# Router as weights on four column groups, and the second expert's weights behind the landing of the first expert's rows

## The chip, the core and the metric

The kernel runs on one core of a Trainium2 chip. The metric is the device time of one execution in microseconds (us). The kernel before takes 1316.21 us, the median of three runs (1314.29 to 1318.43). One further execution was profiled. Its device time is 1313.54 us, and its span, from the first to the last record, is 1311.7 us. All row times below are counted from the start of that span.

## The reference

One layer of a hybrid decoder over 1024 prompt tokens and 8 x 4 sample tokens, of width 1024, all in float32. The first part of the layer (an RWKV-7 recurrence beside windowed attention) is only touched at its loads. What matters here begins with the output projection and the mixture of experts:

```python
x = x + (mixed @ prm['w_out'])                       # 1056 tokens x 1024
h2 = rmsnorm(x, prm['norm_ffn_g'])
pg = softmax(h2 @ prm['w_route_group'] + prm['b_route_group'])         # 4 groups
le = h2 @ prm['w_route_expert'] + prm['b_route_expert']                # 16 experts
# the best group of each token, then the best two of its four experts
y = silu(xb @ w_gate[e]) * (xb @ w_up[e]) @ w_down[e]                  # 1024 -> 512 -> 1024
x = x + sum of the two experts' rows, each by its weight
```

So the router is a product of each token's row h2 (1024 values) with 20 columns: 4 of `w_route_group` and 16 of `w_route_expert`.

## The kernel before

Each engine (TensorE, VectorE, ScalarE, GpSimd, and SyncE, which issues most DMAs) has one instruction stream written out by hand, and semaphores order them. `F32` products need two passes of the array, so each `matmul` or `transpose` leaves two load records and two matmul records where both passes are recorded for it; the counts below are counts of records.

The 1056 tokens are 9 tiles: eight of 128 tokens and one of 32. In the stage that the change touches, TensorE goes through the tiles t = 0 to 8 in this order: the output projection of tile t + 2 (`project`, `w_part`, L1146; the last tile, t = 8, is projected in L1153 on four column groups of the array with 32 tokens each); eight transposes of the normalised rows h2 of tile t (L1214) into PSUM banks 2 and 6; a wait until ScalarE has copied them to `h2T` (`turned_rows`, L1676); and eight products for the router (L1220). In these, a block of `h2T` (128 x 128) is loaded as weights and the 20 columns of `wr20` are moved through, and the eight sum up in bank 3. Beside it, VectorE adds the projected rows to the residual (L2189), ScalarE takes the mean square (`mean_square`, L1666 to L1668), VectorE writes h2 (L2198, L2199), and SyncE stores h2 and x to DRAM (L561, L562). On ScalarE the mean square of tile t + 1 stands ahead of the copies of tile t; for the last tile, four copies (L1686) first bring its projection out of PSUM after t = 6, and its mean square stands behind the copies of t = 7.

After the last router product VectorE works out the choice of experts for all tokens (L2218 to L2262) and, with TensorE (L1292, L1299, L1301), the lists of token numbers for each expert, `idxA` for 128 rows and `idxB` for up to 32 more. GpSimd then gathers the rows of the experts from DRAM with indirect DMAs (L2493), into two slots. Once the first expert's rows have landed (`xg0` at 32: both gathers), TensorE turns them (`turn`, L1239 and L1245), and goes on with gate and up (`gate_up`, L1258), the turn of the next expert, and down (`down`, L1277; L1283 on four column groups). All 16 experts follow this pattern.

An expert's weights are three transfers of 2 MB (`load_expert`, L568), into one of two slots. SyncE issues those of the first two experts together, as soon as h2 and x are stored:

```python
for a in range(2):
    load_expert(EO[a], a)
```

Those of expert n + 2 are issued once `down` of expert n is done. The gathers and the weights use the same 16 DMA engines, on different queues (the gathers on q0, SyncE's transfers on q1).

The router's weights, its bias and the gain `gffn` are loaded by SyncE in L538 to L542, once `ryl_ok` says that the arena below them is free. Behind them on SyncE stand two small outputs, the load of the residual tile 3 (L548), that of the tiles 4 to 7 (L551), and later the stores. `fs_dve` reaches 2 with the product of L2109. At the start of the kernel SyncE loads, under three semaphores, the small LoRA matrices (`lora_in`), the level masks (`level_in`) and the caches and biases (`bias_in`); TensorE, GpSimd, VectorE wait for them.

Of the kernel before, what the change touches and what calls it, by code (L numbers as in the profile page):

```python
# [13 lines left out]
P = 128  # L14
# [49 lines left out]
SEMS = """consts vecs_in lora_in shift_in pad_zero x0 x1 x2 x3 sumsq ms_ok std_ok h_ok hT_ps hT_ok vec_ps vec_ok w0 w1 w2 p_ps p_ok  # L64
shT_ps shT_ok prev_ok dve mixed lora_act lora_ps gates_ok kk_sq kk_ps kk_ms kk_std bonus_in bonus_ps exps scaled
kbt_ok blk_done tails_ok ptail_ps ptail_ok sh_out win_out ptail_out smp_ps smp_ok cum_ok
kvs_ok bias_in level_in level_ok sc_ps sc_ok m_ok e_ok p_norm pt_ps pt_ok ob_ps ob_ok gam_ok gamma_ok
# [4 lines left out]
ln_ok fs_pe fs_dve fs_act f_mean f_yc f_sq f_var f_std f_gate f_sc f_mx wo_in x2_in g_in g_ps g_x2 g_lg  # L72
# [5 lines left out]
def constants():  # L78
# [12 lines left out]
    table = np.concatenate([ident, head_ones, head_ones / HD, strict, m64, eye64, ones, iota, tokid, tokid < TOK, -(TOK + i[:, None]), -4 * (TOK + P + i[:, None] % 32), i[:, None] // 32], axis=1)  # L91
# [27 lines left out]
TABLE = ["ident", "head_ones", "head_mean", "strict", "m64", "eye64", "ones", "iota", "tokid", "valid", "spareA", "spareB", "quarter"]  # L119
TABLE_W = dict(ident=P, head_ones=P, head_mean=P, strict=P, m64=P, eye64=HD, ones=P, iota=CAP, tokid=NT + 1, valid=NT + 1, spareA=1, spareB=1, quarter=1)  # L120
# [4 lines left out]
def program(nc, i, o):  # L125

    ctx = ExitStack()
    with ctx:
# [133 lines left out]
        wr20 = part(F0 + 8192 + 2 * D, KB * 20).rearrange("p (b n) -> p b n", b=KB)  # L262
        rbias = part(F0 + 8192 + 2 * D + 160, 20)
        R0 = F0 + 8192 + 2 * D + 180
# [47 lines left out]
        R0 += 2 * TD  # L312
        OHX = part(R0, 2 * NTT * 3 * NE).rearrange("p (m a e) -> p m a e", m=2 * NTT, a=3)
# [91 lines left out]
        def _(sp):  # L405
# [47 lines left out]
            sp.dma_start(wlora[0:HD, :], i["w_decay_up"][0]).then_inc(s["lora_in"], 16)  # L453
            sp.dma_start(wlora[HD:P, :], i["w_iclr_up"][0]).then_inc(s["lora_in"], 16)
            sp.dma_start(wgate[:, :], i["w_gate_up"][0]).then_inc(s["lora_in"], 16)
            load_w(2)
            sp.dma_start(levelf, i["c_level"]).then_inc(s["level_in"], 16)
# [81 lines left out]
            sp.dma_start(wr20[:, :, 0:NG], i["w_route_group"][0].rearrange("(b p) n -> p b n", p=P)).then_inc(s["g_in"], 16)  # L539
# [35 lines left out]
            for a in range(2):  # L575
                load_expert(EO[a], a)
# [63 lines left out]
        def _(pe):  # L640
# [559 lines left out]
            for t in range(2):  # L1200
                for hf in range(2):
                    last = w_part(t, hf, 7)
                last.then_inc(s["g_ps"], 1)
# [1375 lines left out]
```

## Time and profile before

| | before |
|---|---|
| median of three runs | 1316.21 us (1314.29 to 1318.43) |
| device time of the profiled execution | 1313.54 us |
| its span | 1311.7 us |
| TensorE busy | 1193.5 us (91%) |
| VectorE busy | 468.4 us (36%) |
| ScalarE busy | 360.0 us (27%) |
| mean granted clock of TensorE | 0.957 of full |
| DMA traffic | 176.00 MB, mean 134 GB/s |

The profile page gives busy times over the whole span, and then the span in 40 slices of 32.8 us. The chain of waits follows the work that ended last back to what released each step; its pieces add up to the span, so a piece that is on it and gets shorter shortens the span, as long as nothing else then ends later. The timeline shows instructions in order of time with the idle time before them. In the table of windows the column PEclk is the clock granted to TensorE, 1.00 for 2.4 GHz and 0.50 for 1.2 GHz.

### The profile page before, as it was taken

What the parts mean: (1) busy time and instruction counts of PE and PEld (TensorE: products, weight loads), DVE (VectorE), ACT (ScalarE), POOL (GpSimd) and SP (SyncE); (2) the same over time, 40 slices, a digit from 0 to 9 for tenths busy, and PEclk for the clock granted to TensorE, in tenths of its full rate; (3) what the DMA queues carried; (4) which work ended last, traced back from release to release, by engine and by line L of the source; (5) the groups of instructions that cost most, each with busy time, mean ns of one, the idle gap of its engine ahead of it and who ended that gap; (6) DMA issues with size and microseconds to landing.
All of it is one profiled execution on the core that took longest, in us unless ns stands there. A gap on an engine that the chain in (4) does not pass through costs nothing.

```text
span 1311.7 us, 25299 instructions
## 1 busy us (share of the span) xinstructions
PE 1193.5 (91%) x11136; PEld 852.6 (65%) x11136; DVE 468.4 (36%) x921; ACT 360.0 (27%) x784; POOL 289.1 (22%) x171
## 2 busy tenths in 40 slices
PE   6999999999998877687899998499999999999995
PEld 4666666555665666475544455388887888877884
DVE  4201575377555766666242112500010100011133
ACT  3102555434342554524112112111111011111052
POOL 0000000011101899996000000111111121121203
PEclk8999999999999989988799998599999999999998
DMA  6412000110104000021405102949887788887983
GB/s 204 124 33 69 16 17 18 32 36 21 36 16 59 7 4 3 3 51 38 150 16 187 64 32 93 354 158 277 289 294 260 238 281 270 291 292 252 329 324 127
DMA packets 97194, 176.00 MB, mean 134 GB/s; under 512 B 20403, under 2 KB 42350, under 8 KB 96693
## 3 DMA queue, kind: packets, MB, share of 16 engines
q1 hardware_dynamic: 88548, 152.04, 34.4%
q0 software_dynamic: 8544, 22.51, 6.6%
q8 instruction: 75, 1.23, 0.4%
q14 instruction: 27, 0.21, 0.1%
HBM read 148.89 MB, written 29.06 MB: 136 GB/s over the span
## 4 chain that ended last, share of the span: by engine, by line
PE 83%; DVE 10%; issue 3%; ACT 2%; DMA 1%; SPq 0%; POOLq 0%; POOL 0%; DVEq 0%; ACTq 0%
PE ps L1258 22%; PE ps L674 21%; PE ps L1146 9%; PE ps L1277 9%; PE ps L1283 2%; PE ps L1220 1%; PE ps L753 1%; DVE arena L2018 1%; PE ps L777 1%; PE ps L766 1%; PE ps L1239 1%; PE ps L1245 1%; PE ps L1070 1%; DVE arena L1999 1%; PE ps L1062 1%
## 5 line engine op out<-in xcount | busy, mean ns | idle before, releaser
L674 PE MATMUL ps<-arena 128*128 128x355 f32 x960 | 299.8, 469 | 2.8 <-issue 2.6
L1258 PE MATMUL ps<-arena 128*128 128x160 f32 x2048 | 284.8, 301 | 0.8 <-issue 0.6
L1258 PEld LDWEIGHTS ps<-arena 128*128 128x128 f32 x2048 | 280.9, 191 | 7.1 <-issue 7.1
L674 PEld LDWEIGHTS ps<-arena 128*128 128x128 f32 x960 | 180.3, 191 | 108.3 <-issue 11.2
L1146 PE MATMUL ps<-arena 128*128 128x512 f32 x256 | 120.3, 619 | 0.7 <-DVE arena L2091 0.7
L1277 PE MATMUL ps<-arena 128*128 128x512 f32 x256 | 114.6, 599 | 0.7 <-DVE arena L2273 0.7
L2273 DVE TENSOR_TENSOR arena<-arena,ps 128x160 f32<-128x160 f32 x64 | 20.5, 321 | 254.1 <-ACT arena L1711 254.1
L2493 POOL DMA_INDIRECT arena<-h_dram,idxA x16 | 16.1, 1005 | 430.9 <-DVE idxB L2304 221.8
L1711 ACT ACTIVATE arena<-ps 128x160 f32<-128x160 f32 x64 | 19.5, 304 | 327.0 <-PE ps L1258 327.0
L1146 PEld LDWEIGHTS ps<-arena 128*128 128x128 f32 x256 | 49.3, 198 | 58.6 <-issue 56.8
L2434 POOL TENSOR_TENSOR arena<-arena 128x1024 f32<-128x1024 f32 x4 | 11.4, 2859 | 340.6 <-DVE arena L1895 340.6
L1277 PEld LDWEIGHTS ps<-arena 128*128 128x128 f32 x256 | 47.2, 190 | 54.6 <-issue 53.0
L1368 ACT COPY arena<-ps 128x355 f32<-128x355 f32 x60 | 27.2, 453 | 183.7 <-PE ps L674 183.7
L2486 POOL DMA_INDIRECT x_dram<-arena,rowA x13 | 20.9, 1606 | 94.6 <-DVE arena L2283 94.6
L2454 POOL TENSOR_TENSOR arena<-arena 128x1024 f32<-128x1024 f32 (+4 forms) x40 | 41.0, 1026 | 2.8
L2281 DVE TENSOR_SCALAR arena<-ps,arena 128x512 f32<-128x512 f32 x13 | 9.8, 751 | 87.1 <-PE ps L1277 87.1
L921 PE MATMUL ps<-arena 64*64 64x64 f32 x1280 | 33.1, 242 | 4.3 <-DVE arena L2018 4.3
L2189 DVE TENSOR_TENSOR arena<-arena,ps 128x1024 f32<-128x1024 f32 x8 | 9.8, 1220 | 76.2 <-PE ps L1146 76.2
L1676 ACT COPY arena<-ps 128x512 f32<-128x512 f32 (+1 forms) x18 | 9.1, 553 | 94.7 <-PE ps L1214 94.7
L1435 ACT ACTIVATE arena<-arena 128x256 f32<-128x256 f32 (+1 forms) x64 | 30.9, 485 | 12.6 <-DVE arena L1930 12.6
L1924 DVE SCALAR_TENSOR_TENSOR arena<-ps,arena 128x1024 f32<-128x1024 f32 (+1 forms) x16 | 18.5, 1158 | 42.0 <-PE ps L753 42.0
L2018 DVE COPY_PREDICATED arena<-level,ps 128x512 f32<-128x512 uint8 x32 | 22.7, 710 | 29.6 <-PE ps L933 29.6
(390 smaller groups left out, 1656.9 us busy)
## 6 DMA issues: line engine op xcount, KB each, us to landing
arena<-in_w_exp_gate SPq DMA_DIRECT2D x16, 2048.0 KB, 12.6
arena<-in_w_exp_up SPq DMA_DIRECT2D x16, 2048.0 KB, 17.5
arena<-in_w_exp_down SPq DMA_DIRECT2D x16, 2048.0 KB, 21.9
arena<-in_w_in SPq DMA_DIRECT2D x16, 512.0 KB, 3.8
arena<-in_x_prompt SPq DMA_DIRECT2D x9, 512.0 KB, 4.3
x_dram<-arena SPq DMA_DIRECT2D x9, 512.0 KB, 3.6
h_dram<-arena SPq DMA_DIRECT2D x8, 512.0 KB, 2.6
out_y_prompt<-arena SPq DMA_DIRECT2D x8, 512.0 KB, 2.8
```

The lines of the kernel that those rows point to most:

```text
L674: last = pe.matmul(ps[:, q % 2, 0:m], wr[:, n % 3, k, :], hT[:, k, a:a + m], start=(k == 0), stop=(k == KB - 1))
L921: last = pe.matmul(ps[row(e ^ u), 4 * b + u, j * CH:(j + 1) * CH], LB[row(e), b, u, j, 0:CH], TL[row(e), b, JB * u + j, :], start=True, st ...
L1146: return pe.matmul(ps[0:n, 4 * (t % 2) + hf, :], MX[:, b, t * P:t * P + n], wo[b][:, hf * 512:(hf + 1) * 512], start=(b == 0), stop=(b == 7))
L1258: last = pe.matmul(ps[:, 3 + f % 2, n * CAP:(n + 1) * CAP], w[a][:, k, f * P:(f + 1) * P], xgT[:, a, k, :], start=(k == 0), stop=(k == KB ...
L1277: last = pe.matmul(ps[:, 5 + n, :], eact[:, a, k, 0:P], edown[a][:, k, n * 512:(n + 1) * 512], start=(k == 0), stop=(k == 3))
L1283: last = pe.matmul(ps[j * XB:(j + 1) * XB, 7, 0:TD], eact[:, a, k, P:CAP], edown[a][:, k, j * TD:(j + 1) * TD], start=(k == 0), stop=(k == ...
L1368: act.copy(pT[:, pos, a:a + m], ps[:, q % 2, 0:m]).then_inc(s["p_ok"], 1)
L1435: last = act.activation(sc[:, u % 2, g, a:], sc[:, u % 2, g, a:], ACT.Exp, bias=ast[:, 4 * (u % 2) + g:4 * (u % 2) + g + 1], accum_out=ast ...
L2018: dve.copy_predicated(TL[:, b].rearrange("p (u j) t -> p u j t", u=2), lm(lv, 0, 2 * JB).rearrange("p (u j) t -> p u j t", u=2), ps[:, 4 * ...
L2273: dve.tensor_tensor(eact[:, a, f, :], egl[:, f % 2, :], ps[:, 3 + f % 2, CAP:2 * CAP], ALU.mult).then_inc(s["ac_ok"], 1)
L2454: link(pool.tensor_tensor(stm[:, :, 0:m], stm[:, :, 0:m], stm[:, :, m:2 * m], ALU.add))
L2486: pool.indirect_dma_start(dst, bass.IndirectOffsetOnAxis(rows[:, EO[e]:EO[e] + 1], 0), src[:, e % 2, :], None, compute_op=ALU.add).then_in ...
```

## The change

The router's weights become the stationary side. `wr32` holds 32 columns for each of the eight blocks of 128 rows (20 of them the router's and 12 of zeros, which GpSimd writes). The block k is loaded on column group k mod 4 of the array, and 128 tokens of `h2T` are moved through it; the eight products leave four partial sums of 32 rows each, stacked in the 128 partitions of bank 7. ScalarE copies them to `lT`, and one more product per tile, with `lT` as weights and a 0/1 matrix `stack` (128 x 20) moved, sums the four parts and turns them back, into the same place in bank 3. This product of tile t stands behind the transposes of tile t + 1. `g_lt` counts the partial sums, `g_lt_ok` the copies, and `g_lg` the finished logits as before. The loads of the router's weights and bias, and the write of zeros, wait in addition for `fs_dve` at 2. `wr32` is 96 words wider than `wr20`, and what lies behind it in the arena moves up.

SyncE issues the second expert's weights only when `xg0` is at 32, that is, when both gathers of the first expert have landed. The first expert's are issued as before.

To free two semaphores, the loads of `lora_in` and `level_in` count on `bias_in` as well, and each of the four that wait for one of the three now waits for all 12 transfers. The table of constants grows by the 20 columns of `stack`.

```diff
-        wr20 = part(F0 + 8192 + 2 * D, KB * 20).rearrange("p (b n) -> p b n", b=KB)
-        rbias = part(F0 + 8192 + 2 * D + 160, 20)
-        R0 = F0 + 8192 + 2 * D + 180
+        wr32 = part(F0 + 8192 + 2 * D, KB * 32).rearrange("p (b n) -> p b n", b=KB)
+        rbias = part(F0 + 8192 + 2 * D + 256, 20)
+        R0 = F0 + 8192 + 2 * D + 276
...
+        lT = part(R0, 2 * P).rearrange("p (s t) -> p s t", s=2)
...
             sp.wait_ge(s["ryl_ok"], NB_ * HP)
             sp.dma_start(gffn, i["norm_ffn_g"].to_broadcast([P, D])).then_inc(s["g_in"], 16)
-            sp.dma_start(wr20[:, :, 0:NG], i["w_route_group"][0].rearrange("(b p) n -> p b n", p=P)).then_inc(s["g_in"], 16)
-            sp.dma_start(wr20[:, :, NG:NG + NE], i["w_route_expert"][0].rearrange("(b p) n -> p b n", p=P)).then_inc(s["g_in"], 16)
+            sp.wait_ge(s["fs_dve"], 2)
+            sp.dma_start(wr32[:, :, 0:NG], i["w_route_group"][0].rearrange("(b p) n -> p b n", p=P)).then_inc(s["g_in"], 16)
+            sp.dma_start(wr32[:, :, NG:NG + NE], i["w_route_expert"][0].rearrange("(b p) n -> p b n", p=P)).then_inc(s["g_in"], 16)
...
             for a in range(2):
+                if a:
+                    sp.wait_ge(s["xg0"], 32)
                 load_expert(EO[a], a)
...
-                    pe.wait_ge(s["lora_in"], 48)
+                    pe.wait_ge(s["bias_in"], 16 * 12)
...
+            def logits(t):
+                n = toks(t)
+                pe.wait_ge(s["g_lt_ok"], t + 1)
+                pe.matmul(ps[0:n, 3, t * 20:(t + 1) * 20], lT[:, t % 2, 0:n], T["stack"], start=True, stop=True).then_inc(s["g_lg"], 1)
...
+                if t:
+                    logits(t - 1)
                 pe.wait_ge(s["hT_ok"], 2 * NTT + 2 * t + 2)
                 if t == 0:
-                    pe.wait_ge(s["g_in"], 16 * 5)
+                    pe.wait_ge(s["g_in"], 16 * 5 + 1)
                 for k in range(KB):
-                    last = pe.matmul(ps[0:n, 3, t * 20:(t + 1) * 20], h2T[:, t % 2, k, 0:n], wr20[:, k, :], start=(k == 0), stop=(k == KB - 1))
-                last.then_inc(s["g_lg"], 1)
+                    j = k % 4 * 32
+                    last = pe.matmul(ps[j:j + 32, 7, 0:n], wr32[:, k, :], h2T[:, t % 2, k, 0:n], start=(k < 4), stop=(k >= 4), tile_position=(0, j))
+                last.then_inc(s["g_lt"], 1)
+            logits(NT)
...
                     if t >= 2:
-                        act.wait_ge(s["g_lg"], t - 1)
+                        act.wait_ge(s["g_lt"], t - 1)
...
                 turned_rows(t)
+                act.wait_ge(s["g_lt"], t + 1)
+                if t >= 2:
+                    act.wait_ge(s["g_lg"], t - 1)
+                act.copy(lT[:, t % 2, 0:toks(t)], ps[:, 7, 0:toks(t)]).then_inc(s["g_lt_ok"], 1)
...
-            pool.wait_ge(s["level_in"], 16)
+            pool.wait_ge(s["bias_in"], 16 * 12)
...
+            pool.wait_ge(s["ryl_ok"], NB_ * HP)
+            pool.wait_ge(s["fs_dve"], 2)
+            pool.memset(wr32[:, :, NG + NE:], 0.0).then_inc(s["g_in"], 1)
```

## Rows read from the trace of the kernel before

**Rows 1.** The profile page: TensorE's busy time; its granted clock in 40 slices.
```profile
PE 1193.5 (91%) x11136; PEld 852.6 (65%) x11136; DVE 468.4 (36%) x921; ACT 360.0 (27%) x784; POOL 289.1 (22%) x171
...
PEclk8999999999999989988799998599999999999998
```

**Rows 2.** Waits, TensorE, 880 to 1290 us: in total, times, longest.
```profile
PE ps L1277 <- DVE arena L2273: 0.7, 1, 0.7
```

**Rows 3.** Chain of waits, 680 to 880 us: start us, us, what.
```profile
713.19 15.50 PE ps L1146 x32
...
746.08 0.45 PE ps L1214 x4
...
747.67 1.96 PE ps L1220 x16
749.64 15.52 PE ps L1146 x32
...
768.72 13.82 PE ps L1146 x32
...
803.49 3.59 PE ps L1153 x64
```

**Rows 4.** Views of single lines: ns min/median/max, first and last start in us.
```profile
L1153 PEld LDWEIGHTS ps<-arena x64: 107/110/110, 803.4 to 806.5; 128*32 128x32 f32 x64
...
L1301 PE MATMUL ps<-table,arena x8: 206/218/231, 834.4 to 834.5; 128*32 128x48 f32 x8
...
L1299 PE MATMUL ps<-table,arena x2: 275/292/310, 834.1 to 834.2; 128*128 128x48 f32 x2
```

**Rows 5.** Windows of 1 us: busy time of each engine, PEclk, DMA share, GB/s.
```profile
713.00:714.00 1.00, 1.00 (x3) 0.50 (x3) 1.00 (x1) 0.00 (x0) 0.00 (x0) 0.51 0.00 0
...
767.00:768.00 1.00, 1.00 (x11) 1.00 (x11) 0.00 (x0) 0.97 (x3) 0.00 (x0) 1.00 0.00 0
812.00:813.00 1.00, 0.56 (x3) 0.56 (x3) 0.00 (x0) 1.00 (x2) 0.00 (x0) 0.50 0.00 0
```

**Rows 6.** Timeline, 799 to 821 us: start, us, engine, line [idle before].
```profile
808.67 1.49 ACT L1686 COPY arena<-ps 32x256 f32<-32x256 f32 x4
...
812.27 1.05 ACT L1666 ACTIVATE arena<-arena 32x1024 f32<-32x1024 f32 x1
812.44 3.60 PE L1220 MATMUL ps<-arena 128*128 128x20 f32 x16 [0.73 <-ACT arena L1676]
...
814.01 1.27 DVE L2199 SCALAR_TENSOR_TENSOR arena<-arena,stat 32x1024 f32<-32x1024 f32 x1
...
815.97 1.06 PE L1214 MATMUL ps<-table,arena 32*128 32x32 f32 x8
...
818.53 0.33 DVE L2218 TENSOR_TENSOR arena<-ps,arena 128x160 f32<-128x160 f32 x1 [2.80 <-PE ps L1220]
```

**Rows 7.** Chain of waits, 834 to 880 us.
```profile
837.12 7.61 DMA arena<-h_dram,idxB
...
878.69 1.42 PE ps L1258 x9
```

**Rows 8.** Timeline row; DMA issues (820 us, 837 us, 872 us): us to landing; L568's landings.
```profile
820.97 4.37 SPq L568 DMA_DIRECT2D arena<-in_w_exp_down  x1
...
arena<-in_w_exp_down SPq DMA_DIRECT2D x1, 2048.0 KB, 18.4
...
arena<-h_dram,idxB POOLq DMA_INDIRECT x1, 7.6
...
arena<-h_dram,idxB POOLq DMA_INDIRECT x1, 4.0
...
DMA to landing us min/median/max: 8.9/17.5/29.7
```

**Rows 9.** Timeline, 678 to 693 us: VectorE's L2109 and SyncE's L551.
```profile
678.89 0.28 DVE L2109 TENSOR_TENSOR arena<-yS,ps 128x128 f32<-128x128 f32 x1
...
692.15 0.41 SPq L551 DMA_DIRECT2D arena<-in_x_prompt  x1
```

More of the change, by code:

```diff
@@ L62 @@
 ARENA = 20 * W + KB * W + HP * W1 + 15504
-SEMS = """consts vecs_in lora_in shift_in pad_zero x0 x1 x2 x3 sumsq ms_ok std_ok h_ok hT_ps hT_ok vec_ps vec_ok w0 w1 w2 p_ps p_ok
+SEMS = """consts vecs_in shift_in pad_zero x0 x1 x2 x3 sumsq ms_ok std_ok h_ok hT_ps hT_ok vec_ps vec_ok w0 w1 w2 p_ps p_ok
 shT_ps shT_ok prev_ok dve mixed lora_act lora_ps gates_ok kk_sq kk_ps kk_ms kk_std bonus_in bonus_ps exps scaled
 kbt_ok blk_done tails_ok ptail_ps ptail_ok sh_out win_out ptail_out smp_ps smp_ok cum_ok
-kvs_ok bias_in level_in level_ok sc_ps sc_ok m_ok e_ok p_norm pt_ps pt_ok ob_ps ob_ok gam_ok gamma_ok
+kvs_ok bias_in level_ok sc_ps sc_ok m_ok e_ok p_norm pt_ps pt_ok ob_ps ob_ok gam_ok gamma_ok
 rt_ps rt_act rt_dve r_eye rl_ps rl_ok rc_ps rc_ok rg_ps rg_ok ru_ps ru_ok rx_ps rx_ok rxt_ps rxt_ok rm_ps rm_ok
@@ L71 @@
 sv_out sv_in pool sr_ok sy_out sy_in st_out
-ln_ok fs_pe fs_dve fs_act f_mean f_yc f_sq f_var f_std f_gate f_sc f_mx wo_in x2_in g_in g_ps g_x2 g_lg
+ln_ok fs_pe fs_dve fs_act f_mean f_yc f_sq f_var f_std f_gate f_sc f_mx wo_in x2_in g_in g_ps g_x2 g_lt g_lt_ok g_lg
 h2o0 h2o1 hot hot_ps i_ok n_rounds
@@ L90, in constants @@
     tokid = i[:, None] + P * tile_[None, :]
-    table = np.concatenate([ident, head_ones, head_ones / HD, strict, m64, eye64, ones, iota, tokid, tokid < TOK, -(TOK + i[:, None]), -4 * (TOK + P + i[:, None] % 32), i[:, None] // 32], axis=1)
+    table = np.concatenate([ident, head_ones, head_ones / HD, strict, m64, eye64, ones, iota, tokid, tokid < TOK, -(TOK + i[:, None]), -4 * (TOK + P + i[:, None] % 32), i[:, None] // 32, i[:, None] % 32 == np.arange(20)[None, :]], axis=1)
     levels = []
@@ L116, in constants @@
             "c_sbias": sbias.astype(np.float32)}
-TABLE = ["ident", "head_ones", "head_mean", "strict", "m64", "eye64", "ones", "iota", "tokid", "valid", "spareA", "spareB", "quarter"]
-TABLE_W = dict(ident=P, head_ones=P, head_mean=P, strict=P, m64=P, eye64=HD, ones=P, iota=CAP, tokid=NT + 1, valid=NT + 1, spareA=1, spareB=1, quarter=1)
+TABLE = ["ident", "head_ones", "head_mean", "strict", "m64", "eye64", "ones", "iota", "tokid", "valid", "spareA", "spareB", "quarter", "stack"]
+TABLE_W = dict(ident=P, head_ones=P, head_mean=P, strict=P, m64=P, eye64=HD, ones=P, iota=CAP, tokid=NT + 1, valid=NT + 1, spareA=1, spareB=1, quarter=1, stack=20)
 VECS = ["norm_mix_g", "mu_shift", "w_decay0", "w_iclr0", "k_k", "k_a", "r_k", "lnx_g", "lnx_b", "attn_norm_g"]
@@ L452, in _ @@
             sp.dma_start(shin[:, :], i["state_shift"][0]).then_inc(s["shift_in"], 16)
-            sp.dma_start(wlora[0:HD, :], i["w_decay_up"][0]).then_inc(s["lora_in"], 16)
-            sp.dma_start(wlora[HD:P, :], i["w_iclr_up"][0]).then_inc(s["lora_in"], 16)
-            sp.dma_start(wgate[:, :], i["w_gate_up"][0]).then_inc(s["lora_in"], 16)
+            sp.dma_start(wlora[0:HD, :], i["w_decay_up"][0]).then_inc(s["bias_in"], 16)
+            sp.dma_start(wlora[HD:P, :], i["w_iclr_up"][0]).then_inc(s["bias_in"], 16)
+            sp.dma_start(wgate[:, :], i["w_gate_up"][0]).then_inc(s["bias_in"], 16)
             load_w(2)
-            sp.dma_start(levelf, i["c_level"]).then_inc(s["level_in"], 16)
+            sp.dma_start(levelf, i["c_level"]).then_inc(s["bias_in"], 16)
             for dst, src in ((kc, "cache_win_k"), (vc, "cache_win_v")):
@@ L782, in s_cache @@
             def s_cache(n):
-                pe.wait_ge(s["bias_in"], 16 * 8)
+                pe.wait_ge(s["bias_in"], 16 * 12)
                 pe.wait_ge(s["sa_act"], 1 + n)
@@ L1955, in _ @@
             link(dve.memset(pn[:, :, 0:1], 0.0))
-            dve.wait_ge(s["bias_in"], 16 * 8)
+            dve.wait_ge(s["bias_in"], 16 * 12)
             for k in range(NU + 1):
@@ L2193, in _ @@
                 if t == 0:
-                    dve.wait_ge(s["g_in"], 16 * 5)
+                    dve.wait_ge(s["g_in"], 16 * 5 + 1)
                 if t >= 2:
```

## The prediction

> **What bounds the kernel now.** I read the page first. TensorE is busy 91% of the span, and its granted clock is full in most slices but not in those around 700 to 760 us and 790 to 850 us [rows 1]. The next view is the waits of TensorE behind 880 us: in the whole phase of the experts the longest is 0.7 us, once [rows 2]. That phase is TensorE's own work, and the change does not touch it; whatever is won ahead of it moves its start and is kept. So the question is what stands on the chain of waits between 700 and 880 us. There the chain is nearly all TensorE: projection of a tile, transposes, a wait for ScalarE's copies, and the router's 16 records, again and again [rows 3]. Then comes VectorE's choice of experts, and then one DMA, the gather of the first expert's last rows, at 7.61 us [rows 7]. The change aims at the router's records and at this gather.
>
> **The router, tiles 0 to 5.** The 16 records of a tile take 1.96 us on the chain [rows 3], 0.123 us each, for only 20 moved columns; they are paid for by the loads of 128 columns of weights. After the change 32 columns are loaded and 128 moved, on four column groups. The nearest row is L1153, which also has loads of 32 columns on four groups, but moves 256: 64 records in 3.59 us [rows 3], 0.056 us each. Half the columns should take half of that, 0.028 us, if columns set the price: 16 x 0.028 = 0.45 us. The other bound comes from eight records of L1301, 48 columns wide, whose starts lie within 0.1 us [rows 4], about 0.015 us each, which shows that the loads of 32 columns alone allow 0.24 us. From above, 16 x 0.056 = 0.90 us. I take 0.6 us, the half of L1153 and 0.15 us for going into the column groups and out of them, as an estimate: the 3.59 us of L1153 hold two such changes and leave little more than that over its smooth part. The gain is 1.96 - 0.6 = 1.37 us a tile (bounds 1.07 and 1.6), and six tiles (0 to 5) are followed by a projection, so that it stays on the chain: 8.2 us (6.4 to 9.6).
>
> The added product of each tile costs two records with 128 columns of weights; the like of L1299 has two in about 0.4 us [rows 4]. It stands behind the next tile's transposes, where TensorE waits for ScalarE anyway: from the end of the transposes at 746.53 to the router at 747.67 it is idle for 1.14 us [rows 3]. So it costs nothing for tiles 0 to 7; without that cover it would be 0.4 us a tile, 3 us in all. ScalarE's added copy (128 x 128, below 0.3 us) comes before its mean square of a later tile, which is not needed for more than 10 us, since a projection of 13.8 us stands in between.
>
> **The clock.** The same 32 records of a projection take 15.50 and 15.52 us behind tiles 0 and 2, and 13.82 us behind tile 3 (and also behind 1 and 4) [rows 3]. The windows show why: at 713 us and again at 751 us the granted clock is 0.5, that is 1.2 GHz, for 3.4 us, while it stays at 1.0 behind the other tiles [rows 5]. What TensorE did before these falls is always the same: transposes, 1.14 us of idling, and 2 us of products that move 20 columns. After the change the idling has a product in it, and the router takes a third of the time with four groups at work on 128 columns, so the stretch of little work shrinks from 3.6 us to about 2.2 us. I expect the two falls to go: 1.68 + 1.70 = 3.4 us. The bounds are 0 (they stay, or come at other tiles instead) and 3.4.
>
> **The last tiles.** Here no projection is left to hide anything. Before, from the start of the transposes of tile 6 (807.01) to VectorE's first step on the logits (818.53) it is 11.5 us [rows 6]. I go through it anew. The router of tile 6 ends 1.4 us earlier, but ScalarE now copies its parts (0.3 us) before the four copies of L1686 (1.49 us), which end at 4.25 instead of 3.15 us from the start; only then does it copy the transposes of tile 7, to 5.3 us, just as before. The router of tile 7 ran at the low clock in 3.60 us [rows 6]; now it ends at about 6.0 to 6.4 us. That gain is not kept: the mean square of tile 8 used to run beside it, and now stands behind the copy of tile 7's parts on ScalarE. It begins at 6.3 to 6.7 us, takes 1.5 us, and VectorE's two steps another 1.5 (1.27 of them L2199), so the transposes of tile 8 begin at 9.3 to 9.7 us instead of 8.96 us. Behind them, the copies take 1.4 us, the router 0.5 instead of 1.04 us, then the new copy 0.35 us and the last product 0.4 us, which nothing hides any more. Sum: 12.0 to 12.5 us against 11.5. The tail loses 0.8 us (0.5 to 1.3). The falls of the clock in the tail I leave as they are: at 812 us it is at 0.5 [rows 5], and stretches of waiting remain.
>
> **The gather.** The two experts' weights, 12.6 MB, are issued from 820 us on and fill the DMA engines until about 855 us. The gather of `idxB` is issued at 837.12 and lands after 7.6 us; the same gather at 872 us, with no weights under way, lands after 4.0 us [rows 7, 8]. After the change only the first expert's 6.3 MB stand ahead. Its last transfer lands 18.4 us after its issue at 820.97, at 839.4 [rows 8]; since the stores of the last tile come 0.4 us later against VectorE's steps, at 839.8. Until then the gathers share, and from then they are alone: some 0.4 MB of the 0.66 MB are left, 1 us at the engines' rate, and then the landing. I put the landing of `idxB` at 841.4 instead of 844.7, a gain of 3.3 us. Bounds: 3.6 us (the undisturbed 4.0) from above, and 2 us if the first expert's transfers hold the rows up longer. The first expert's weights have landed before gate and up need them, 3.6 us after the rows.
>
> The second expert's weights are then issued at 841.4 us, 21 us later than before. They are needed at 878.69 - 3.3 = 875.4 us [rows 7], 34 us later. With nothing queued ahead, the three of the first expert took 18.4 us to the last landing, and the longest landing of any is 29.7 us, which was with 12.6 MB queued [rows 8]. So nothing waits for them, with 4 us to spare in the worst case and 15 us in the likely one. Behind the new wait on SyncE stand only the third expert's weights, which wait for the first `down` anyway, and TensorE and GpSimd need nothing of that queue sooner.
>
> **The waits for 12 transfers and for `fs_dve`.** `fs_dve` is at 2 at 679.2 us [rows 9], 39 us after the router's weights were loaded before. Five issues and two small outputs take about 5 us on SyncE, so the residual tile 3 is issued near 685 us and not at 675.6, and lands by 689; L551 behind it waits for VectorE until 692.15 us [rows 9] and is not moved. The router's weights land near 689 us, and TensorE wants them at 711 us, VectorE the bias of `g_in` near 698 us. Cost 0; the cover is 9 us. The merged waits cost 0 too: the last of the 12 loads is issued at 40 us and the level masks and LoRA weights are used behind 240 us. GpSimd has been idle since 613 us when it writes the zeros. The table's 10 KB more are below what the vectors' loads behind it take.
>
> **The sum.** 8.2 + 3.4 - 0.8 + 3.3 = 14.1 us. Against the profiled execution, 1313.54 - 14.1 = 1299.4 us; the median of the runs is 2.7 us above it, so 1316.2 - 14.1 = 1302.1 us.
>
> **Rivals.**
> (a) The falls of the clock stay or move to other tiles. For it: they depend on where they strike among like tiles (two of six before). Against it: the stretch of little work is shorter by a third. 10.7 us, 1305.5 us.
> (b) Loads set the router's price, not columns. Each load of 32 columns lasts 0.110 us [rows 4]; if they could not overlap, 16 would take 1.76 us, the gain would be 0.2 us a tile, and the total 14.1 - 8.2 + 1.2 = 7.1 us, 1309.1 us. Against it: L1153 has 64 of them in 3.59 us, so they do overlap.
> The Trainium skill ("TensorE: Matmul & The Clock Gate", Back-to-back issue gap) gives about 81 ns for each pair of load and matmul in a sustained stream at 128 moved columns; that would be an estimate of 1.3 us a tile and a gain of 4 us in place of 8.2. By that rule the time would be some 4 us above my forecast; no row before shows 128 columns on four groups.
> (c) The gather waits for something other than the weights, and its 7.6 us stay. For it: its own issue and the second expert's gathers are near. Against it: 4.0 us when alone. 10.8 us, 1305.4 us.
> (d) Slower: the second expert's weights come too late for its `gate_up` at 875.4 us. Every us beyond 34 us from issue to landing is paid in full, and the kernel is slower than before from 48 us on; at 52 us it would be 1302.1 + 18 = 1320 us. Against it: no landing beyond 29.7 us.
> (e) Slower by nothing, faster by nothing: several of (a) to (c) at once, near 1312 us.
>
> **How the numbers follow.** Forecast 0.62, (a) 0.14, (b) 0.10, (c) 0.06, (d) 0.03, (e) 0.05. The forecast's own bounds are 6.4 to 9.6 for the router, 0.5 to 1.3 for the tail, 2 to 3.6 for the gather; with some 2 us for the runs' spread they reach from 1298 to 1307, and that holds (a) and (c) as well, some 8 in 10. A measurement of this kernel can tell about 0.3%, 4 us. Faster by more than that: the forecast, (a), (b), (c): 0.92. Same: (e), 0.05. Slower: (d), 0.03.
>
> **What the next profile would show.** The chain has 16 records of the router in 0.5 to 0.7 us a tile (0.9 or more speaks for (b)). All projections behind tiles 0 to 4 take 13.8 us (15.5 anywhere is (a)). From the transposes of tile 6 to VectorE's first step it is 12.0 to 12.5 us. The gather of `idxB` lands 4 to 5 us after its issue (7.6 is (c)). TensorE does not wait for the second expert's weights; if it does, (d). A wait of TensorE or VectorE for `g_in` near 700 us, or idling between the column groups and the projection, would make the sum wrong in a place that I put at nothing.

## The result, and the profile after

The changed kernel takes 1303.81 us in the median of six runs (1301.74 to 1310.42), the kernel before, measured beside it, 1317.29 us (1313.31 to 1318.95). The ratio is 0.9931 with a 95% interval of 0.9908 to 0.9954: 9.1 us less of 1316.21, between 6.1 and 12.1. That makes 1307.1 us against a forecast of 1302.1 us, 0.1 us beyond the upper end of its range (1298 to 1307 us). The profiled execution has a span of 1301.7 us, 10.0 us below that of before. The same changed kernel run once more later (e11 below) gave 0.9915 (0.9886 to 0.9943).

The page of the kernel after, first the row of busy times, then TensorE's granted clock in 40 slices:

```profile
PE 1182.3 (91%) x11154; PEld 843.4 (65%) x11154; DVE 468.9 (36%) x921; ACT 361.8 (28%) x793; POOL 289.1 (22%) x172
...
PEclk9999999999999989888899998599999999999998
```

TensorE is busy for 11.2 us less than in [rows 1]. The chain of waits of the kernel after, 680 to 875 us (start us, us, what), holds the rest of the story; L1150 is the projection, L1232 the router's parts, L1223 the transposes, L1157 the projection of the last tile, L2235 VectorE's first step on the logits, L1305 the lists of tokens, L1271 gate and up:

```profile
694.16 17.43 PE ps L1150 x40
...
713.19 0.64 PE ps L1232 x16
713.84 13.93 PE ps L1150 x32
...
794.71 3.45 PE ps L1157 x64
798.17 0.60 PE ps L1223 x4
...
804.40 1.05 ACT arena L1679 x2
...
810.05 0.34 DVE arena L2235
...
820.88 5.27 PE ps L1305 x36
...
829.62 5.20 DMA arena<-h_dram,idxB
...
838.52 20.02 PE ps L1271 x128
```

The router takes 0.64 us a tile where [rows 3] has 1.96 us. Each of the five projections behind tiles 0 to 4 takes 13.93 us: none is at 15.5 us as two were in [rows 3], and none is at the 13.82 us of the others. The gather of `idxB` lands after 5.20 us, not 7.61 us [rows 7].

The same chain of the kernel before, beside [rows 3] and [rows 7] (L1292 are the lists of tokens, L1258 gate and up):

```profile
692.17 17.43 PE ps L1146 x40
...
807.08 0.60 PE ps L1214 x4
...
829.37 4.29 PE ps L1292 x36
...
848.44 19.84 PE ps L1258 x128
```

A stage that starts and ends at the same work in every version makes the kernels comparable. I use the stretch from the transposes of tile 0 to the first expert's gate and up. Before, it goes from 709.60 (the last piece of the projection ahead of the transposes of tile 0 begins at 692.17 and takes 17.43 us) to 848.44: 138.84 us. After, it goes from 711.59 to 838.52: 126.93 us, which is 11.91 us less. The remaining difference lies outside it: the stage begins 1.99 us later after, and the experts' phase behind it is within 0.1 us of what it was.

### The profile page after: what moved, and what is told of

The parts are those of the page before. It is cut to its first block, busy times and chain, and to the rows that moved or that the text cites. A ratio compares the mean times of both kernels' runs of the same rounds, so it can differ in the third digit from the quotient of the medians.

```text
span 1301.7 us, 25353 instructions
## 1 busy us (share of the span) xinstructions
PE 1182.3 (91%) x11154; PEld 843.4 (65%) x11154; DVE 468.9 (36%) x921; ACT 361.8 (28%) x793; POOL 289.1 (22%) x172
## 4 chain that ended last, share of the span: by engine, by line
PE 83%; DVE 10%; issue 3%; ACT 3%; DMA 1%; SPq 0%; POOLq 0%; POOL 0%; DVEq 0%; ACTq 0%
PE ps L1271 22%; PE ps L678 21%; PE ps L1290 9%; PE ps L1150 9%; PE ps L1296 2%; PE ps L757 1%; DVE arena L2035 1%; PE ps L781 1%; PE ps L770 1%; PE ps L1252 1%; PE ps L1074 1%; PE ps L1258 1%; PE ps L937 1%; PE ps L946 1%; DVE arena L2016 1%
## 5 line engine op out<-in xcount | busy, mean ns | idle before, releaser
L1271 PE MATMUL ps<-arena 128*128 128x160 f32 x2048 | 285.1, 301 | 0.6 <-issue 0.6
L1271 PEld LDWEIGHTS ps<-arena 128*128 128x128 f32 x2048 | 281.0, 191 | 6.9 <-issue 6.9
L1150 PE MATMUL ps<-arena 128*128 128x512 f32 x256 | 115.1, 597 | 0.7 <-DVE arena L2108 0.7
L1290 PE MATMUL ps<-arena 128*128 128x512 f32 x256 | 114.6, 599 | 0.7 <-DVE arena L2290 0.7
L1150 PEld LDWEIGHTS ps<-arena 128*128 128x128 f32 x256 | 47.4, 190 | 56.8 <-issue 55.1
L1013 PEld LDWEIGHTS ps<-arena 64*64 64x64 f32 x240 | 13.2, 145 | 29.3 <-DVE arena L2055 17.4
```

Source lines behind the costliest of these rows:

```text
L1150: return pe.matmul(ps[0:n, 4 * (t % 2) + hf, :], MX[:, b, t * P:t * P + n], wo[b][:, hf * 512:(hf + 1) * 512], start=(b == 0), stop=(b == 7))
L1271: last = pe.matmul(ps[:, 3 + f % 2, n * CAP:(n + 1) * CAP], w[a][:, k, f * P:(f + 1) * P], xgT[:, a, k, :], start=(k == 0), stop=(k == KB ...
L1290: last = pe.matmul(ps[:, 5 + n, :], eact[:, a, k, 0:P], edown[a][:, k, n * 512:(n + 1) * 512], start=(k == 0), stop=(k == 3))
```

## The experiments

Stage lengths below are all from the transposes of tile 0 to the first gate and up, each from one profiled execution. Where no ratio is given (e5 to e8 and e10), the kernel was run once, and the profiled execution is that run.

**e1: the changed kernel without the wait for the rows.**

```diff
             for a in range(2):
-                if a:
-                    sp.wait_ge(s["xg0"], 32)
                 load_expert(EO[a], a)
```

> The changed kernel without its wait for the first expert's rows: both experts' weights are issued together, as before. Theory (the router and the gather are two separate gains): the sum of the trace after is about -11 us for the router with the clock, +0.4 for the tail, -2.4 for the gather, so this kernel should be 7 to 9 us faster than before, and 2 to 3 us slower than the changed kernel, with the gather of idxB landing about 7.6 us after its issue again. All projections behind tiles 0 to 4 take 13.8 to 13.9 us. Rival (the gather is not slowed by the second expert's weights): it is as fast as the changed kernel, and idxB lands after 5 us.

Measured: ratio 0.9915 (0.9887 to 0.9944). Chain of waits of e1:

```profile
710.62 13.93 PE ps L1148 x32
...
825.72 6.90 DMA arena<-h_dram,idxB
...
836.32 20.33 PE ps L1269 x128
```

The stage goes from 708.37 to 836.32, 127.95 us: 10.9 us shorter than before without the wait. The expectation was right on the gather being slow again (6.90 us) and wrong on how much the wait adds: the changed kernel's stage is only 1.0 us shorter than this one, not 2 to 3 us, and the two ratios cannot be told apart.

**e2: the kernel before with the wait alone.**

```diff
             for a in range(2):
+                if a:
+                    sp.wait_ge(s["xg0"], 32)
                 load_expert(EO[a], a)
```

> The kernel before with only the wait for the first expert's rows ahead of the second expert's weights. Theory: idxB lands after 5 us and not 7.6 us, the kernel is 2 to 3 us faster than before, and one to three of the projections behind tiles 0 to 5 take about 15.5 us, since the router is the old one. Rival (the wait is worth nothing or makes the second expert late): within 0.5 us of before, or a wait of TensorE for the second expert's weights.

Measured: ratio 0.9952 (0.9932 to 0.9972), 6.3 us less (3.7 to 9.0). Chain of waits of e2:

```profile
713.84 15.20 PE ps L1148 x32
732.61 15.52 PE ps L1148 x32
...
829.72 5.27 PE ps L1294 x36
...
838.71 3.65 DMA arena<-h_dram,idxB
...
846.19 19.30 PE ps L1260 x128
```

The wait alone brings the gather's own row from 7.61 to 3.65 us, 4.0 us. The stage, 709.97 to 846.19, is 136.22 us, only 2.6 us shorter than before. The row overstates the gain: the token lists took 5.27 us here against 4.29 us, so that this gather was issued later. The measure that holds is from VectorE's first step on the logits to the landing of `idxB`: 26.2 us before (818.53 to 844.73), 23.5 us here (818.89 to 842.36). On top of the router the wait gains 1.0 us by the same measure: 25.8 us in e1, 24.8 us after and 24.9 us in e11. So the two halves of the change don't add up. The times give the wait alone 6.3 us, and even the lower end of their interval, 3.7 us, is above the 2.6 us of the stage; where the rest lies is open.

A part of the reason is in the next view.

The timeline row in which SyncE issues the last of the first expert's weights, of the kernel after, and the us from that issue to landing:

```profile
813.46 3.96 SPq L570 DMA_DIRECT2D arena<-in_w_exp_down  x1
...
arena<-in_w_exp_down SPq DMA_DIRECT2D x1, 2048.0 KB, 19.3
```

Before, this issue stood 2.44 us behind VectorE's first step on the logits (818.53 and 820.97, [rows 6, 8]); after, 3.41 us (810.05 and 813.46). The weights wait for the stores of tile 8, which wait for its mean square. The first of these stores was issued 3.2 us ahead of VectorE's first step before and 2.7 us ahead of it after, which is half of the 1.0 us; the other half is that the weights were issued 3.77 us behind the last store's issue and not 3.30 us, for which no run shows a cause. Then the transfer itself took 19.3 us to its landing, where it took 18.4 us before. It took 19.2 to 20.2 us in all six executions with the new products in which all of the first expert's weights are issued ahead of the gather (after, e1, e5, e6, e10, e11), and 18.4 to 18.6 us in the four without them; the cause is open too. So the first expert's weights land at 832.76, 3.1 us behind the issue of the gather at 829.62. In the kernel before, where the second expert's weights follow at once, the first's landed at 839.4, 2.3 us behind the issue at 837.12.

**e3: what is left of the change without the new products and without the wait.** The router multiplies as before, by 20 of the 32 columns.

```diff
-                if a:
-                    sp.wait_ge(s["xg0"], 32)
...
-                    j = k % 4 * 32
-                    last = pe.matmul(ps[j:j + 32, 7, 0:n], wr32[:, k, :], h2T[:, t % 2, k, 0:n], start=(k < 4), stop=(k >= 4), tile_position=(0, j))
-                last.then_inc(s["g_lt"], 1)
-            logits(NT)
+                    last = pe.matmul(ps[0:n, 3, t * 20:(t + 1) * 20], h2T[:, t % 2, k, 0:n], wr32[:, k, 0:20], start=(k == 0), stop=(k == KB - 1))
+                last.then_inc(s["g_lg"], 1)
...
-                act.copy(lT[:, t % 2, 0:toks(t)], ps[:, 7, 0:toks(t)]).then_inc(s["g_lt_ok"], 1)
```

> What is left of the change without the router's new products and without the wait for the rows: merged semaphores, the wider table and wr32 in the arena, the loads of the router's weights behind fs_dve, the zeros. The router multiplies as before, by 20 of the 32 columns. Theory (the 2 us that the trace after loses ahead of 693 us are the clock's falls striking at other places in this one execution, not the change): the ratio to before is 1.000 within 0.002, and the stages ahead of 693 us come out within 2 us of before, either way. Rival (the merged waits or the table cost time): 1.5 to 3 us slower than before, and the start of the output projection's last part comes 2 us later in its trace.

Measured: ratio 0.9996 (0.9974 to 1.0018). Chain of waits of e3:

```profile
712.11 15.52 PE ps L1148 x32
...
765.96 15.52 PE ps L1148 x32
...
836.13 7.05 DMA arena<-h_dram,idxB
```

The stage is 138.34 us (708.54 to 846.88), as before within 0.5 us. The merged semaphores, the wider table, the moved arena and the wait for `fs_dve` cost nothing that shows. The timeline of the kernel after agrees: the load of the residual tile 3 (L550) is issued at 684.05, 10 us before L553, the load of tiles 4 to 7, which still goes as soon as VectorE allows it.

```profile
684.05 0.36 SPq L550 DMA_DIRECT2D arena<-in_x_prompt  x1
694.13 0.41 SPq L553 DMA_DIRECT2D arena<-in_x_prompt  x1
```

**e4: the kernel before, unchanged.**

> The kernel before, unchanged, as a kernel of its own: how far a comparison of a kernel with itself is from 1, and how far stages differ between two profiled executions of one program. Theory (the clock's falls strike differently from one execution to the next): ratio 1.000 within 0.002; the falls behind the router's tiles come at other tiles or in another number than behind tiles 0 and 2, each at 1.7 us, and the stages ahead of 693 us differ by 1 to 3 us. Rival (they are fixed by the program): again 15.5 us behind tiles 0 and 2 alone, and the stages ahead within 0.5 us.

Measured: ratio 0.9996 (0.9973 to 1.0019). Chain of waits of e4:

```profile
688.53 17.43 PE ps L1146 x40
...
709.73 15.31 PE ps L1146 x32
...
745.99 15.52 PE ps L1146 x32
...
825.73 4.20 PE ps L1292 x36
...
833.41 7.34 DMA arena<-h_dram,idxB
```

The stage is 138.48 us (705.97 to 844.45), 0.4 us from the first profiled execution, but it begins 3.6 us earlier (688.53 against 692.17 for its last projection piece). So one program's stages ahead of it differ by that much between executions. The falls came behind tiles 0 and 2 again, which the rival expected; but in e3 and e2, whose TensorE work here is the same, they came behind tiles 0 and 3, and 0 and 1. All four have two falls among the five, one of them behind tile 0; the place of the other is not fixed.

**e10: the old router's products beside the new ones.** They go into columns of bank 3 that nobody reads.

```diff
+                for k in range(KB):
+                    pe.matmul(ps[0:n, 3, 256:276], h2T[:, t % 2, k, 0:n], wr32[:, k, 0:20], start=(k == 0), stop=(k == KB - 1))
                 for k in range(KB):
                     j = k % 4 * 32
```

> The changed kernel, in which TensorE also does the old router products (16 records of 20 moved columns a tile) ahead of the new ones, into columns of bank 3 that nobody reads. It tells what of the old router goes with the falls of the clock. Theory (the falls come with the long stretch of light work: transposes, idling and products of 20 columns): about 2.6 us a tile for the router's lines instead of 0.64, and the falls are back, so that one to three of the projections behind tiles 0 to 5 take 15.2 to 15.6 us. Rival (the new products at the end of the stretch are enough to hold the clock): all of them take 13.8 to 13.9 us.

Measured: 1327.39 us in one run. Chain of waits of e10 (L1231 the old products, L1234 the new):

```profile
715.86 16.48 PE ps L1150 x32
...
733.93 1.96 PE ps L1231 x16
735.90 0.57 PE ps L1234 x16
...
754.54 15.63 PE ps L1150 x32
...
792.37 15.63 PE ps L1150 x32
```

With the old products back, the falls are back: 16.48, 15.63 and 15.63 us behind tiles 0, 2 and 4, and 13.93 behind the other two. The new products at the end of the stretch don't hold the clock. Together with the eight profiled executions without the old products (after, e1, e5 to e9, e11), in which all 40 projections took 13.93 us, and the four with the old ones alone (before, e2 to e4), two falls in each, this shows that the falls went with the old router's products. It does not tell whether their few moved columns do it or the time that they take: from the transposes to the next projection it is 3.6 us before and 4.1 us in e10, with falls, and 2.2 us after and 2.7 us in e6, without. No run has a long way there without the old products.

**e6: the new products twice.**

```diff
-                for k in range(KB):
+                for k in [*range(KB), *range(KB)]:
                     j = k % 4 * 32
```

> The changed kernel with the eight products of the router's parts issued twice for each tile (the second time over the first, the same result). It measures the price of 16 more records. Theory (moved columns set the price): 16 x 0.027 = 0.43 us more, 1.07 us a tile instead of 0.64. Rival 1 (loads or a fixed price per record, 0.64 / 16 = 0.040 us): 1.28 us a tile. Rival 2 (loads of 0.110 us do not overlap, or the Trainium skill's 81 ns a pair): 1.9 us or more. The projections stay at 13.9 us in all three.

Measured: chain of waits of e6:

```profile
719.95 1.08 PE ps L1232 x32
```

Sixteen more records cost 0.44 us, 0.0275 us each. The loads of 0.110 us one behind the other, 0.081 us a pair and 0.040 us a record are out by this number. That columns set it takes a second row, since e6 adds columns and records alike: L1153, with the same loads and 256 columns, takes 0.056 us a record [rows 3], twice as much. It is also a fourth of what the full array takes: the projection moves 512 columns a record in 0.432 us (13.82 / 32, [rows 3]), which is 0.108 us for 128. The other 0.20 us of the 0.64 are not in the price of a record and are paid once a tile; that they are the way into the column groups is argued. The rows of the last projection agree: it takes 3.59 us [rows 3] behind products on the full array and 3.45 us (L1157) behind the new ones, 0.14 us less.

**e5: ScalarE's order of the last tiles.** The four copies of the last projection ahead of the copy of tile 6's parts, the mean square of tile 8 ahead of the copy of tile 7's.

```diff
                 turned_rows(t)
-                act.wait_ge(s["g_lt"], t + 1)
-                if t >= 2:
-                    act.wait_ge(s["g_lg"], t - 1)
-                act.copy(lT[:, t % 2, 0:toks(t)], ps[:, 7, 0:toks(t)]).then_inc(s["g_lt_ok"], 1)
                 if t + 1 == NT - 1:
...
                 if t + 1 == NT:
                     mean_square(NT)
+                act.wait_ge(s["g_lt"], t + 1)
+                if t >= 2:
+                    act.wait_ge(s["g_lg"], t - 1)
+                act.copy(lT[:, t % 2, 0:toks(t)], ps[:, 7, 0:toks(t)]).then_inc(s["g_lt_ok"], 1)
```

> The changed kernel with ScalarE's order of the last tiles changed: the four copies of the last tile's projection ahead of the copy of tile 6's parts, and the mean square of tile 8 ahead of the copy of tile 7's parts. Theory (the tail is longer than before because ScalarE's copies of the parts stand ahead of the mean square of tile 8): from the transposes of tile 6 to VectorE's first step on the logits it is 11.88 us in the changed kernel and should be 10.4 to 10.8 us here. Rival (the tail is set by TensorE and the last copy and product): 11.7 to 12.0 us.

Measured: span 1299.2 us. Chain of waits of e5 (L1679 is the mean square of tile 8):

```profile
796.65 0.60 PE ps L1223 x4
...
801.07 1.16 ACT arena L1679 x2
...
806.83 0.34 DVE arena L2235
```

From the transposes of tile 6 to the logits it is 10.18 us, a little below what was expected, against 11.88 us in the kernel after: the mean square begins 4.42 us behind the transposes instead of 6.23 us. So ScalarE's order was what made the tail longer. But the stage is only 1.4 us shorter (125.48 us, 710.07 to 835.55). The gather took 6.34 us, 1.1 us more than after, while the token lists took 4.37 us, 0.9 us less: it was issued earlier, and the first expert's weights were under way beside it for longer. From the logits to the landing of `idxB` it is 25.0 us.

**e7: the first expert's down weights also behind its rows.**

```diff
...
-            for a in range(2):
-                if a:
-                    sp.wait_ge(s["xg0"], 32)
-                load_expert(EO[a], a)
+            load_expert(EO[0], 0, slice(0, 2))
+            sp.wait_ge(s["xg0"], 32)
+            sp.wait_ge(s["w0"], w_total(18) + 32)
+            load_expert(EO[0], 0, slice(2, 3))
+            load_expert(EO[1], 1)
...
-                pe.wait_ge(s[f"w{a}"], WBASE[a] + 24 * g + (48 - 24 * a))
+                pe.wait_ge(s[f"w{a}"], WBASE[a] + (32 if a == 0 and first else 24 * g + (48 - 24 * a)))
...
+                if first:
+                    pe.wait_ge(s["w0"], WBASE[0] + 48)
```

> The changed kernel with the third transfer of the first expert's weights (down, 2 MB) also behind the landing of its rows; down waits for it by itself. Theory (the gather of idxB takes 5.2 us in the changed kernel because the first expert's last transfer is still under way): it lands 3.6 to 4.1 us after its issue, 1.1 to 1.6 us earlier, and nobody waits for down's weights, which land some 9 us after and are needed 20 us after. Rival (the 5.2 us are the gather's own): 5.0 to 5.3 us again.

Measured: span 1300.4 us. Chain of waits of e7, and the landing of the down weights:

```profile
829.59 3.92 DMA arena<-h_dram,idxB
...
arena<-in_w_exp_down SPq DMA_DIRECT2D x1, 2048.0 KB, 9.0
```

The gather lands after 3.92 us, and nobody waits for the down weights. The stage is 124.87 us (712.33 to 837.20), 2.1 us shorter than after; 1.3 us of it is the gather, 0.8 us the token lists, which here took 4.49 us instead of 5.27. So what was left of the gather's delay was the first expert's own third transfer. Here the shorter lists count, because nothing holds up the gather that follows them: from the logits to the landing of `idxB` it is 22.7 us. In e11 the lists took the same 4.49 us, and it is 24.9 us, 0.1 us more than after.

**e8: both experts' weights behind the rows.**

```diff
             for a in range(2):
-                if a:
+                if not a:
                     sp.wait_ge(s["xg0"], 32)
                 load_expert(EO[a], a)
```

> The changed kernel with the weights of both first experts behind the landing of the first expert's rows: no weights at all are under way when the rows are gathered, and the first expert's weights come late. It measures the gather alone and the price of late weights. Theory: idxB lands 3.6 to 4.1 us after its issue; gate and up of the first expert wait for the weights, which take 18.4 us to the last landing, so gate and up begin about 13 to 14 us later than in the changed kernel, and all of it is in the span (some 1315 us); the second expert's weights, which land some 34 us after the rows, still come before their gate and up. Rival (a late transfer is made up for later, since the experts' phase has slack): the span is less than 5 us above that of the changed kernel.

Measured: span 1319.5 us. Chain of waits of e8:

```profile
830.69 3.79 DMA arena<-h_dram,idxB
...
835.63 21.42 DMA arena<-in_w_exp_down
857.19 19.16 PE ps L1271 x128
```

The gather without any weights beside it takes 3.79 us. The span is 17.8 us longer than after; the stage, 713.45 to 857.19, is 143.74 us, 16.8 us longer, and the other 1.9 us lie ahead of it, less 0.9 us behind it. The last transfer landed 21.4 us after its issue instead of my 18.4, which is where the cost goes above the 13 to 14 us expected; the gathers of the next experts ran beside it, and that they are the cause is argued. Late weights are not made up for: gate and up begin 0.1 us after the landing, and only 0.9 us of the 16.8 came back. So the mechanism of rival (d) exists, shown here on the first expert's weights; in the changed kernel nothing waits for the second's.

**e9: e5 and e7 together.**

> The changed kernel with both amendments: ScalarE's order of the last tiles, and the first expert's down weights behind the landing of its rows. From the last full-length projection piece of 17.43 us to the first gate and up it was 144.4 us in the changed kernel, 142.9 with the order alone and 142.3 with the down weights alone. Theory (they take different pieces of the chain, and the shorter tail exposes more of the first expert's weights to the gather, which the other amendment takes away): 140.4 to 141.5 us here, idxB landing 3.6 to 4.1 us after its issue, ratio to before 0.987 to 0.991, 2.5 to 4 us ahead of the changed kernel. Rival (only one of the two counts): 142.3 us or more, and less than 2 us ahead of the changed kernel.

Measured: ratio 0.9919 (0.9893 to 0.9946), span 1294.9 us. Chain of waits of e9:

```profile
692.00 17.43 PE ps L1151 x40
...
825.16 3.72 DMA arena<-h_dram,idxB
...
832.58 19.16 PE ps L1272 x128
```

The stage is 123.15 us (709.43 to 832.58), 3.8 us shorter than after. Expected were 140.4 to 141.5 us counted from the start of the 17.43 us piece; it is 140.58. In the profile the two amendments add up (1.4 and 2.1 us alone), with some luck: the tail takes 9.6 us and not the 10.2 us of e5, since the clock fell only at the end of it. The expected ratio, 0.987 to 0.991, was missed. In the times the amendments don't show: the ratio of e9 is 0.9919, that of the changed kernel measured beside it 0.9915, each uncertain by 0.003. A version that beats the changed kernel is seen in the trace, and not shown by the times.

**e11: the changed kernel again.**

> The changed kernel itself once more, beside its amended form and on another day's chip. Theory: ratio to before 0.990 to 0.993; no fall of the clock behind tiles 0 to 5; 11.9 us from the transposes of tile 6 to the logits; idxB lands 5 us after its issue; the stages ahead of 693 us lie anywhere within 3 us of the first execution, since only the clock's falls move them. Rival (the 2.0 us lost ahead of 693 us belong to the changed program): the last projection piece of 17.43 us begins at 694 us or later again.

Measured: ratio 0.9915 (0.9886 to 0.9943), 11.2 us less. Chain of waits of e11:

```profile
694.45 17.43 PE ps L1150 x40
...
821.21 4.49 PE ps L1305 x36
...
829.17 6.07 DMA arena<-h_dram,idxB
...
838.94 19.02 PE ps L1271 x128
```

The issue of the first expert's last weights in e11, and the us to their landing:

```profile
813.80 4.23 SPq L570 DMA_DIRECT2D arena<-in_w_exp_down  x1
...
arena<-in_w_exp_down SPq DMA_DIRECT2D x1, 2048.0 KB, 19.9
```

The stage is 127.06 us (711.88 to 838.94), 0.1 us from that of the kernel after, though its parts differ: token lists 0.8 us shorter, gather 0.9 us longer. The two belong together. The weights land at 833.7 and `idxB` at 835.24, 1.5 us behind them (2.1 us after): as long as the first expert's weights are under way, a gather that is issued earlier does not land earlier. The gather was expected after 5 us. The start of the first piece, 694.45, is what the rival said; I come back to it below.

## Why the prediction was right or wrong

The forecast was 14.1 us; the change brought 9.1 us in the first measurement and 11.2 us in the second, 10.0 us in the profiled execution. The direction was right, and so were the mechanisms of the router and the clock. The step that failed is the gather: its gain was put at 3.3 us and is 1.4 us. A further 2.0 us ahead of the stage, which the sum did not have, stay open. Point by point, from the traces of before and after:

**Router, tiles 0 to 5: 8.2 forecast, 7.5 found.** The tile's price was right, 0.64 us for 0.6; e6 and L1153 together show that columns set it. The gain is 6 x 1.32 = 7.9 us. Two small terms were missing: the projection behind each new router takes 13.93 instead of 13.82 us, five times 0.11, and L1157 3.45 instead of 3.59 us. I counted the way out of the column groups in the router's lines; it is paid in the next line too.

**Clock: 3.4 forecast, 3.4 found.** 1.68 + 1.70 us [rows 3] are gone in all executions. e10 shows the old products as the cause; by the length of the way between two projections or by their few columns is open. Rival (a) is out.

**Tail: 0.8 forecast, 0.4 lost.** From 11.45 (807.08 to 818.53) to 11.88 us. The step was right in kind, as e5 shows: the mean square of tile 8 stands behind the copy of tile 7's parts. The loss was sized a little too high (bounds 0.5 to 1.3): the granted clock is still 1.00 in the router of tile 7, at 803 us, and 0.50 only from 806 us.

**Gather: 3.3 forecast, 1.4 found. This is the step that failed.** The forecast let the first expert's weights land 21.3 us behind VectorE's first step on the logits and `idxB` 1.6 us later, at 22.9 us instead of 26.2 us. After, the weights land at 22.7 us and `idxB` at 24.8 us. Three terms are short: the weights are issued 1.0 us later against that step (2.44 to 3.41 us), not 0.4; their last transfer takes 19.3 us, not 18.4; and the gather lands 2.1 us behind them, not 1.6. In e11 they are 1.0 us, 19.9 us and 1.5 us, with the same end (24.9 us). e2 and e1 show what the error comes to: the wait is worth 2.6 us of the stage by itself and 1.0 us on top of the new router. e7 shows what holds the gather up: with the first expert's last transfer out of its way it lands in 3.92 us. Rival (c) is out.

**Not a term of its own: the token lists.** L1305 took 5.27 us for 4.29 us of L1292, partly at the low clock (0.50 until 826 us after, until 832 us before). It would be easy to book 2.4 us won at the gather (7.61 to 5.20 us) and 1.0 us lost here. e11 contradicts that: with lists of 4.49 us the gather takes 6.07 us, and the stage is the same. The 1.4 us above are the two rows together.

These give 7.5 + 3.4 - 0.4 + 1.4 = 11.9 us, the whole change of the stage.

**Ahead of the stage, 2.0 us lost: open.** By the chains of before and after, the projection's last piece begins at 692.17 and at 694.16. What the program does there differs by the merged waits, the table, the moved loads and the zeros, and e3, which has them all, starts at 691.11 and measures 0.9996 (0.9974 to 1.0018). So they are not the cause. In the four executions without the new router the piece ends at 706.0 to 710.0 us; in the nine with it (e10 too) at 708.4 to 718.4 us, two of them within the range of the four, a third 0.1 us beyond it. The same program (after and e11, and e1, e5 to e9, equal up to this point but for where their code lies) spreads over 10 us, so most of it is scatter. Whether a part of 1 or 2 us belongs to the changed program is not settled. If it does, it would explain why the times show some 10 us and the stage 11.9.

**The range.** Its upper end of 1307 us is not what its terms give: 6.4 + 3.4 - 1.3 + 2.0 = 10.5 us, less the 2 us of spread, is a gain of 8.5 us and 1307.7 us, and the clock's own lower bound of 0 is not in it. The measured 1307.1 us lies between the two. A range from one execution also has no room for a stretch ahead of the stage that differed by 3.6 us between two executions of the same kernel.

**Nothing for the merged waits, `fs_dve` and the zeros: right** (e3, and the timeline of after: 10 us of cover on SyncE). **Second expert's weights: right.** (The DMA engines before were full until about 860 us, not 855; nothing hangs on it.) TensorE has one wait behind 870 us, 0.7 us, the same as in [rows 2]:

```profile
PE ps L1290 <- DVE arena L2290: 0.7, 1, 0.7
```

**Rival (b)** is out by e6: 0.0275 us a record, where a load lasts 0.110 us. The Trainium skill's figure in "TensorE: Matmul & The Clock Gate" (Back-to-back issue gap), 81 ns for a pair of load and matmul at 128 columns, would have given a gain near 4 us for six tiles; the run has 27.5 ns where each load is of 32 columns and four groups work at once. The Trainium skill's page "TensorEngine Tiling (Array Packing)", Key Properties, says that changing the tiling mode drains the array; the 0.20 us paid once a tile (e6), the 0.11 us behind and the 0.14 us that L1157 saves agree with a price for that. The forecast had all of this in one term of 0.15 us.

## What to carry to other kernels

When a product has few output columns and many rows, load the few columns as weights on column groups and move the rows: the price is then that of the moved columns divided by the groups (0.0275 us a record for 128 columns in float32 here) and not that of full weight loads, and the array's clock may hold through a stretch where it used to fall, as it did here. When a transfer is on the chain, count what of its own kind still stands ahead of it after the change: holding back the next expert's weights was worth 2.6 us of the stage alone and 1.0 us with the other half of the change. Measure such a gain from a point ahead of the transfer to its landing: the transfer's own row said 4.0 us (7.61 and 3.65) and 1.7 us (6.90 and 5.20), because it also changes with the time of issue. And a step that is added on an engine with time to spare (ScalarE's copy) belongs behind the work of that engine that others wait for, which took 1.7 us off the tail in e5.

## What the runs showed of the hardware

The falls of the granted clock came twice in each of the four executions with the old router alone, once behind tile 0 and once behind another tile, and in none of the 40 projections without its products. A tile's turn on the column groups takes 0.20 us in its own lines that 16 more records don't add, and 0.11 us in the projection behind. The gather of `idxB` lands 3.7 to 3.9 us after its issue with no weights under way (e7, e8, e9) and after 6.9 to 7.6 us with those of two experts under way (before, e1, e3, e4). Two profiled executions of the same program begin this stage up to 3.6 us apart (before and e4), while the stage itself repeats within 0.5 us (0.1 us for after and e11); comparing stages resolved differences of 1 us that ratios with intervals of 0.005 did not.
